# Seven block products for the last down projection of a float32 decoder trunk, its weight sums made by adding transfers

## The reference

```python
def swiglu_ffn(h, w_gu, w_down):
    g, u = jnp.split(h @ w_gu, 2, axis=-1)
    return (jax.nn.silu(g) * u) @ w_down
...
        x = x + 0.5 * swiglu_ffn(rmsnorm(x, n_ffn2[i]), ffn2_w_gu[i], ffn2_w_down[i])
    return rmsnorm(x, n_final)
```

## Time and profile before

| | us |
|---|---|
| median of 3 runs (1934.22 to 1935.02) | 1934.61 |
| the profiled execution | 1933.99 |
| its span, first to last instruction | 1932.2 |

### The profile page before, as it was taken

The page is one execution under the profiler, slowest core; times in us unless marked ns, Lnnn a source line. Parts: engine busy times, 40 slices in busy tenths (PEclk is TensorE's granted clock), DMA queues, the critical chain, the costliest instruction groups (busy, mean ns, idle before and its releaser), DMA issues.

```text
span 1932.2 us, 31908 instructions
## 1 busy us (share of the span) xinstructions
PE 1923.7 (100%) x12020; PEld 1740.5 (90%) x12020; DVE 1347.7 (70%) x2111; ACT 964.4 (50%) x1612; POOL 329.0 (17%) x331
## 2 busy tenths in 40 slices
PE   9999999999999999999999999999999999999998
PEld 7998998888898889989998998999898889989997
DVE  7865875687765658847866985687487569837854
ACT  7542554355554546524544653365356446524543
POOL 2200212100112121101201120121312123401200
PEclk9999999999999999999999999999999999999999
DMA  6734974323443627736943683695353427847932
GB/s 181 164 109 117 181 153 138 109 67 108 131 128 114 173 87 171 157 103 150 186 111 119 135 169 98 140 189 132 110 179 121 109 70 180 173 153 164 188 109 87
DMA packets 385097, 263.82 MB, mean 137 GB/s; under 512 B 19314, under 2 KB 367600, under 8 KB 384992
## 3 DMA queue, kind: packets, MB, share of 16 engines
q1 hardware_dynamic: 303840, 209.22, 36.4%
q0 software_dynamic: 72224, 51.19, 17.3%
q10 hardware_dynamic: 8928, 2.11, 0.5%
HBM read 251.99 MB, written 10.49 MB: 136 GB/s over the span
## 4 chain that ended last, share of the span: by engine, by line
PE 97%; DVE 1%; issue 1%; ACT 1%; DMA 0%; ACTq 0%
PE ps L434 19%; PE ps L435 18%; PE ps L436 18%; PE ps L1068 14%; PE ps L1067 14%; PE ps L1066 14%; DVE w_lo L2118 0%; ACT w_hi L1447 0%; PE ps L992 0%; PE ps L926 0%; DVE sums L2876 0%; DMA x_tok<-in_x 0%; DVE sums L2896 0%; DVE up L3065 0%; PE ps L1192 0%
## 5 line engine op out<-in xcount | busy, mean ns | idle before, releaser
L2118 DVE TENSOR_TENSOR w_lo<-raw,w_hi 128x512 fp32r<-128x512 f32 (+5 forms) x367 | 397.1, 1096 | 299.7 <-ACT w_hi L1447 299.3
L1447 ACT ACTIVATE w_hi<-raw 128x512 fp32r<-128x512 f32 (+5 forms) x367 | 342.6, 951 | 298.5 <-PE ps L436 255.1
L1067 PE MATMUL ps<-s_lo,w_hi 128*128 128x256 f32 x1248 | 353.2, 283 | 0.0
L1068 PE MATMUL ps<-s_hi,w_lo 128*128 128x256 f32 x1248 | 353.2, 283 | 0.0
L1066 PE MATMUL ps<-s_hi,w_hi 128*128 128x256 f32 x1248 | 353.2, 283 | 0.0
L1068 PE MATMUL ps<-h_hi,w_lo 128*128 128x256 f32 x936 | 264.9, 283 | 0.0
L1067 PE MATMUL ps<-h_lo,w_hi 128*128 128x256 f32 x936 | 264.9, 283 | 0.0
L1066 PE MATMUL ps<-h_hi,w_hi 128*128 128x256 f32 x936 | 264.8, 283 | 0.0
L1066 PEld LDWEIGHTS ps<-s_hi,w_hi 128*128 128x128 f32 x1248 | 239.6, 192 | 0.0
L1067 PEld LDWEIGHTS ps<-s_lo,w_hi 128*128 128x128 f32 x1248 | 239.6, 192 | 0.0
L1068 PEld LDWEIGHTS ps<-s_hi,w_lo 128*128 128x128 f32 x1248 | 239.6, 192 | 0.0
(11 more groups left out here) (406 smaller groups left out, 3789.8 us busy)
## 6 DMA issues: line engine op xcount, KB each, us to landing
raw<-in_ffn_w_gu SPq DMA_DIRECT2D x110, 512.0 KB, 5.0
raw<-in_ffn_w_down SPq DMA_DIRECT2D x36, 768.0 KB, 4.4
outer_even<-in_ffn_w_gu SPq DMA_DIRECT2D x70, 256.0 KB, 3.2
outer_even<-in_ffn_w_gu POOLq DMA_DIRECT2D x70, 256.0 KB, 5.4
raw<-in_ffn_w_gu SPq DMA_DIRECT2D x64, 256.0 KB, 6.1
raw<-in_x_w_kv SPq DMA_DIRECT2D x16, 1024.0 KB, 6.1
raw<-in_ffn_w_down SPq DMA_DIRECT2D x24, 640.0 KB, 4.2
outer_odd<-in_ffn_w_gu SPq DMA_DIRECT2D x54, 256.0 KB, 3.6
```

The source lines that it names most:

```text
L1067: nc.tensor.matmul(to, hi[:, kk, :], right_lo, start=False, stop=False, skip_group_check=True)
L1068: last = nc.tensor.matmul(to, lo[:, kk, :], right_hi, start=False, stop=kk == KH - 1, skip_group_check=True)
L1447: return nc.scalar.activation(out_ap, in_ap, ACT.Copy, **kw)
L2118: return nc.vector.tensor_tensor(out_ap, value, hi.bitcast(F32), ALU.subtract)
```

## The change

The last block's 20 mixed slots become one run, and its down projection comes once, behind them, as seven block products. The operands are split in two along tokens (256 and 256), rows (11 and 11) and columns (512 and 512); each product is 2 token tiles x 11 rows x 3 matmuls of 512 columns, cut in six tiles of two rows (the last of one). The gated values stay in float32 (mid); their forms are made as sums by VectorE and split tile by tile, four tiles ahead. The weight forms: P1, P2 and P3 are plain; P5, P6 and P4 take w_chain, to which POOL adds one block after the other by accumulating transfers of up to four rows; P7 takes P3's raw rows with one more addition. ScalarE copies P1's first eight rows into w_chain. Each product is taken into x by one to two scaled additions for each token tile (POSTS). The additions of POOL for slots l = 10 to 19 now follow the loads of x by token on its queue.

```diff
-    TOKEN_GROUPS = ((0, 3), (3, 3), (6, 3), (9, 2))
-    LAST_GROUP = len(TOKEN_GROUPS) - 1
+    RUNS = (2, 2, 2, 1)
...
+    DOWN_ORDER = (P1, P2, P5, P6, P3, P7, P4)
+    DOWN_GROUPS = ((0, 4), (4, 4), (8, 3))
+    DOWN_TILES = ((0, 2), (2, 2), (4, 2), (6, 2), (8, 2), (10, 1))
+    PER = len(DOWN_TILES)
+    LAST_TILE = PER * PRODUCTS
+    POSTS = {P1: ((0, 0, 1), (1, 0, 1)), P2: ((0, 0, -1), (1, 0, -1)), P5: ((2, 1, 1), (3, 1, 1)),
+             P6: ((0, 1, -1), (1, 1, -1)), P3: ((0, 1, 1), (1, 1, 1)),
+             P7: ((2, 1, -1), (3, 1, -1), (2, 0, 1), (3, 0, 1)), P4: ((2, 0, -1), (3, 0, -1))}
...
+    def run_slots(n, part):
+        return range(FC) if RUNS[n] == 1 else range(part * HALF, (part + 1) * HALF)
+
+    def first_mixed(n, part):
+        return max(run_slots(n, part)[0], PLAIN_FIRST[n])
+
...
+            w_chain = last_run.enter_context(nc.sbuf_tensor("w_chain", [P, HALF, SEQ], F32))
...
+        w_rest = region("w_rest", 32 * KB, [P, 3, SEQ])
+        final_gain = region("final_gain", 38 * KB, [P, D])
+        mid = region("mid", 44 * KB, [P, FC, SEQ])
+        first_hi_forms = region("first_hi_forms", 88 * KB, [P, 4, TH], F32R)
+        first_lo_forms = region("first_lo_forms", 92 * KB, [P, 4, TH], F32R)
...
+        DOWN_BANK = {P1: (4, 5), P6: (4, 5), P7: (4, 5), P2: (6, 7), P5: (0, 1), P3: (0, 1), P4: (2, 3)}
+        RAW_AT = {(P1, 0): 0, (P1, 1): 1, (P2, 0): 2, (P2, 1): 3, (P2, 2): 4, (P3, 0): 5, (P3, 1): 6}
...
+            def load_down_products():
                 down = io.ffn2_w_down[1].rearrange("(k p) n -> p k n", p=P)
-                for half in range(2):
-                    for g, (row, nrows) in enumerate(TOKEN_GROUPS):
-                        w = at["down", 3, part, half, g].slot
-                        first = part * HALF + row
-                        sp.wait_ge(sig.w_lo_ready, w - 1)
-                        sp.dma_start(wide(raw[:, w % 2])[:, 0:nrows, :],
-                                     down[:, first:first + nrows, half * SEQ:(half + 1) * SEQ])\
-                          .then_inc(raw_loaded[w % 2], 16)
+                def load_rows(i, g):
+                    k0, nrows = DOWN_GROUPS[g]
+                    first, half = k0 + (HALF if i in (P2, P3) else 0), int(i == P3)
+                    r = RAW_AT[i, g]
+                    sp.dma_start(rows_of(i, g), down[:, first:first + nrows, half * SEQ:(half + 1) * SEQ])\
+                      .then_inc(raw_loaded[raw_slot(r)], 16)
+                sp.wait_ge(sig.w_lo_ready, SLOTS - 1)
+                load_rows(P1, 0)
+                sp.wait_ge(sig.w_lo_ready, SLOTS)
+                load_rows(P1, 1)
+                sp.wait_ge(sig.product_done, PRODUCTS_DONE)
+                k0, nrows = DOWN_GROUPS[2]
+                sp.dma_start(w_chain[:, k0:k0 + nrows, :], down[:, k0:k0 + nrows, 0:SEQ]).then_inc(sig.t1_loaded, 16)
+                for g in range(2):
+                    sp.wait_ge(sig.w_lo_ready, SLOTS + tile(P1, 2 * g + 1) + 1)
+                    sp.wait_ge(sig.x_scaled_ready, CHAIN_COPIED + g + 1)
+                    load_rows(P2, g)
+                sp.wait_ge(sig.form_lo_ready, FORMS_DONE)
+                sp.wait_ge(sig.t1_loaded, REST_LOADED + 16)
+                sp.dma_start(w_rest[:], down[:, HALF + k0:HALF + k0 + nrows, SEQ:]).then_inc(sig.t1_loaded, 16)
+                for g, freed in enumerate((P2, P2, P2)):
+                    sp.wait_ge(sig.w_lo_ready, SLOTS + tile(freed, 2 * g + 1) + 1)
+                    if g == 0:
+                        load_rows(P2, 2)
+                    else:
+                        load_rows(P3, g - 1)
...
-                pool.dma_start(final_gain[:], io.n_final.unsqueeze(0).broadcast_to([P, D])).then_inc(sig.gain_loaded, 16)
...
+            def add_down_sums():
+                down = io.ffn2_w_down[1].rearrange("(k p) n -> p k n", p=P)
+                pool.wait_ge(sig.product_done, PRODUCTS_DONE)
+                pool.wait_ge(sig.form_lo_ready, FORMS_DONE)
+                pool.dma_start(final_gain[:], io.n_final.unsqueeze(0).broadcast_to([P, D])).then_inc(sig.gain_loaded, 16)
+                for g, (k0, nrows) in enumerate(DOWN_GROUPS):
+                    if g < 2:
+                        pool.wait_ge(sig.x_scaled_ready, CHAIN_COPIED + g + 1)
+                    else:
+                        pool.wait_ge(sig.w_lo_ready, SLOTS + tile(P1, 2 * g + 1) + 1)
+                    pool.dma_start(w_chain[:, k0:k0 + nrows, :], down[:, k0:k0 + nrows, SEQ:], accum_op=ALU.add)\
+                        .then_inc(CHAIN_ADDED[g][0], 16)
+                for g, (k0, nrows) in enumerate(DOWN_GROUPS):
+                    pool.wait_ge(sig.w_lo_ready, SLOTS + tile(P5, 2 * g + 1) + 1)
+                    pool.wait_ge(CHAIN_ADDED[g][0], CHAIN_ADDED[g][1] + 16)
+                    pool.dma_start(w_chain[:, k0:k0 + nrows, :], down[:, HALF + k0:HALF + k0 + nrows, SEQ:],
+                                   accum_op=ALU.add).then_inc(CHAIN_ADDED[g][0], 16)
+                for g, (k0, nrows) in enumerate(DOWN_GROUPS):
+                    pool.wait_ge(sig.w_lo_ready, SLOTS + tile(P6, 2 * g + 1) + 1)
+                    pool.wait_ge(CHAIN_ADDED[g][0], CHAIN_ADDED[g][1] + 32)
+                    pool.dma_start(w_chain[:, k0:k0 + nrows, :], down[:, HALF + k0:HALF + k0 + nrows, 0:SEQ],
+                                   accum_op=ALU.add).then_inc(CHAIN_ADDED[g][0], 16)
+                for g, (k0, nrows) in enumerate(DOWN_GROUPS):
+                    pool.wait_ge(sig.w_lo_ready, SLOTS + tile(P3, 2 * g + 1) + 1)
+                    pool.dma_start(rows_of(P3, g), down[:, k0:k0 + nrows, SEQ:], accum_op=ALU.add)\
+                        .then_inc(T3_ADDED[g][0], 16)
...
-            add_run(3, 1)
+            for l in range(C + 2, mixed_count(3, 0)):
+                add_outer(3, 0, l)
...
+            def down_products():
+                last_slot = len(mixed_slots) - 1
+                for k in range(LAST_TILE):
+                    i, q = DOWN_ORDER[k // PER], k % PER
+                    pe.wait_ge(sig.form_lo_ready, FORMS_DONE + k + 1)
+                    pe.wait_ge(sig.w_lo_ready, SLOTS + k + 1)
+                    if q == 0:
+                        if i == P2:
+                            pe.wait_ge(sig.mixed_dve_step, dve_step(last_slot, C11_TAKEN))
+                            pe.wait_ge(sig.mixed_act_step, act_step(last_slot, P5_TAKEN))
+                        if i in (P5, P4):
+                            pe.wait_ge(sig.mixed_dve_step, dve_step(last_slot, C21_TAKEN))
+                        if i in (P6, P3, P7):
+                            pe.wait_ge(sig.evacuated, evacuated_after({P6: P1, P3: P5, P7: P6}[i]))
+                    hi, lo = down_w(w_hi, k), down_w(w_lo, k)
+                    left_hi, left_lo = down_forms(first_hi_forms, s_hi, k), down_forms(first_lo_forms, s_lo, k)
+                    nrows = DOWN_TILES[q][1]
+                    for j in range(2):
+                        to, ts = ps[:, DOWN_BANK[i][j], :], slice(j * P, (j + 1) * P)
+                        for n in range(nrows):
+                            fresh = i in (P1, P2, P5, P4) and (q, n) == (0, 0)
+                            nc.tensor.matmul(to, left_hi[:, n, ts], hi[:, n, :], start=fresh, stop=False,
+                                             skip_group_check=True)
+                            nc.tensor.matmul(to, left_hi[:, n, ts], lo[:, n, :], start=False, stop=False,
+                                             skip_group_check=True)
+                            last = nc.tensor.matmul(to, left_lo[:, n, ts], hi[:, n, :], start=False,
+                                                    stop=(q, n) == (PER - 1, nrows - 1), skip_group_check=True)
                         last.then_inc(sig.part_done, 1)
...
+                        down_form_hi(0)
+                        down_hi(0)
...
+                    for k in (2, 3):
+                        down_form_hi(k)
+                    down_hi(2)
+                    high_silu(m, s)
+                    return
...
+            def down_products():
+                copied = {4: 0, 5: 1}
+                nc.scalar.activation(idle[:], eps[:], ACT.Sqrt)
+                down_hi(3)
+                for k in range(LAST_TILE):
+                    if k in copied:
+                        g = copied[k]
+                        k0, nrows = DOWN_GROUPS[g]
+                        act.wait_ge(sig.product_done, PRODUCTS_DONE)
+                        hi_part(w_chain[:, k0:k0 + nrows, :], rows_of(P1, g)).then_inc(sig.x_scaled_ready, 1)
+                    if k >= 4:
+                        down_hi(k)
+                    if k + 4 < LAST_TILE:
+                        down_form_hi(k + 4)
+                    if k == 18:
+                        for tt in (0, 1):
+                            token_squares(early(tt), tt, evacuated_after(P2) - 1 + tt)
+                    if k in (34, 35):
+                        tt = k - 34
```

(93 more changed lines are left out.)

330 lines of the change are left out of this document (201 added, 129 removed).

## The result

The changed kernel takes 1944.27 us (median of 5, 1942.74 to 1944.87) beside 1934.61 for the kernel before: 1.0048 times as long, 95% interval 1.0035 to 1.0062. It is **slower by 0.5%**, where 1929.1 was forecast, and the time lies 1.3 us above the range. The profiled execution has a span of 1942.6 us, 10.4 more than before.

The account below looks back on a forecast made before the run. It took TensorE, busy without a gap, as the bound: 66 fewer matmuls (-14.96) + 4.0 + 3.3 + 0 + 2.2 = -5.5 us, from a median of 1934.6 to 1929.1 us. Range 1923 to 1943.

Parts of the forecast that it names:

- Entering the down stage: Start of the down stage: PE stalls 1.3 at tile 4, 1.1 plus 0.9 at tile 6; 3.3 us, 1.5 to 6.
- Rival (2): As P2 begins: plain loads share engines packet by packet with additions, stalls 13.2 rather than 3.3 us; 1939; chance 0.11.
- Slot 9: Slot l = 9: additions for l = 10, behind x's loads, land at 1703.5 and stall PE 4.0 us, 1.5 to 6.
- Rival (4): Slot 9's pause: TensorE's clock falls, 3.5 us at 1.2 GHz costing about as much again; 1932.5; chance 0.10.
- Rival (3): Slot 9: the x loads do not hold the additions up, so the 4.0 us go; 1925.1; chance 0.15.
- The transfers' term: Additions from P5 on: 165 ns per 2 KB packet, hidden below 195, so 0 us; 16 us late at 256.
- Rival (1): Tiles 30 to 35: additions cost by byte, 256 ns a packet, and P7's chain falls behind; 1945; chance 0.17.
- VectorE: Down products: VectorE's work exceeds 14.96 by 1 to 3 us in P6 and P3, covered by four-tile lead; 0 us.
- The end: After PE's last matmul: tokens 2 and 3 end only 3 matmuls apart, token 3 taken later; +2.2 us, 1.5 to 3.

Follow-up runs that it names:

- no_first_sums: Changed kernel with P5's three first additions into w_chain cut to 16 columns of one row each (P5, P6, P4 multiply other weights): 1930.41 us.
- rest_late: Changed kernel with w_rest's 768 KB load issued behind P3's loads instead of between P2's second and third: 1937.86 us.
- x_late: Changed kernel with the additions for slot l = 10 issued ahead of the loads of x instead of behind them: 1937.91 us.
- no_later_sums: Changed kernel with the nine additions for P6, P4 and P7 cut to 16 columns of one row each (these multiply other weights): 1943.62 us.
- ahead_early_p3: Changed kernel with l = 10 additions ahead of x, w_chain loaded directly, P2's first and last rows loaded earlier, P4's last tiles by token: 1927.99 us.
- direct_rest: Changed kernel with w_rest's load behind P3's, w_chain filled by loads instead of ScalarE's copies, P2's first two loads earlier: 1935.75 us.
- two_queues: Changed kernel with half of each of P2's first two loads issued by ScalarE on its own queue: 1941.86 us.
- wait_x_rest_tail: Changed kernel with P5's additions held for P2's first two loads, l = 10 additions ahead of x, w_rest behind P3's loads, P4's last tiles by token: 1932.68 us.

## Why the prediction was wrong

**The failed step is "Entering the down stage"**: 3.3 us forecast, 15.6 measured (11.7 of waits, counted from start to start of the matmuls, 3.9 of lower clock and restart). Its two stalls were right: 1.3 and 2.0 at tiles 4 and 6, measured 1.1 and 1.8, and of the second the additions made 0.7, by no_first_sums, where 0.9 was put. What it lacked stands two and four tiles further on, 5.1 and 3.7 us at tiles 8 and 10. I stopped at these 0.9 us for "the first addition into w_chain beside it", where the step should have followed every load of SyncE's queue up to P2's third: 1 MB, w_rest's 768 KB, 768 KB, each packet behind one of an addition.

**Rival (2) is what happened**, by its mechanism. That its 13.2 us of stalls came near the 11.7 us is partly luck: it put 6.2, 2.8 and 2.9 us at tiles 6, 8 and 10, where 1.8, 5.1 and 3.7 came, and it had no w_rest ahead of the third load, without which tile 10 did not wait (rest_late). I gave it 0.11, and the evidence I held against it was misread: raw loads of 4.9 and 4.7 us with and without additions are medians over stretches; in the first the additions' queue held the engines 40% of the time, in pieces of 256 KB, so many of a load's packets may have met none (I did not count them). A median over a mixed stretch can't speak for a megabyte beside a megabyte. Its 1939 fell short of 1944.27 mostly by the clock: 1.5 us in slot 9 and 3.5 in the stage.

**Slot 9** was right in place and size: 4.0 forecast, 3.65 measured and, by x_late, due to x; VectorE took the addition up at 1704.96 in an execution whose slots start 1.57 us later, so at 1703.4 by the time axis of before, where 1703.5 was put. Rival (4) came true beside it rather than instead of it: the clock fell behind this pause, for the 3.5 us that it put (no row of before showed that length), and this cost 1.5 us. Its price of 3.5 was reckoned wrong: a stretch at half the clock loses half its length, not as much again. The prediction let rivals (2) and (4) exclude each other, but a rival that makes pauses can bring the clock with it. Rival (3) is refuted.

**The transfers' term**, 0, was right in this kernel: 183 ns (165 taken, 195 the point where it turns), no gap in P6 and P7, and no_later_sums the same as after. Rival (1) is refuted at this price. The Trainium skill (Collectives: The Full Stack, "The bandwidth ceiling: the fold count and why AG ≠ RS ≠ AR") has the reduction of a collective ring read two sources where a copy reads one, at half the rate. Carried over to these additions, as the prediction did, that is an estimate of 2 x 92.4 = 185 ns, and the trace's 183 agrees. But the term looked only at the chain from P5 on, and that it held owes something to luck: with most of P2's waits gone, P5 and P6 come some 15 us earlier and PE waits there as well (ahead_early_p3).

**VectorE**, 0, held: no wait of PE in the fifth stretch, with VectorE busy for 64.6 of 74.7 us. **The end**, 2.2, was 2.0. **Not in the sum** were 1.0 us ahead of P4 in the last slot, which every variant shows. In the kernel after VectorE works without a pause from 1808.52 until it has made what P4 waits for, and two of its operations there are new, the low part of a first form and a sum into mid, 1.0 us together; what happens without them was not tried.

## What to carry to other kernels

When transfers that add are moved beside loads that a tensor engine waits for, write down every load on every queue with its size and its due time, and let them share packet for packet: a cheap load then moves at the dear one's pace. Order each queue by due time, and look for transfers that stand ahead of an urgent one for no reason (x ahead of the additions: 5 us; w_rest ahead of P2: 4.6 us). A pause can have a lower clock behind it, and not every pause has, so compare pauses and clock apart; and saved work counts only as far as the transfers that pay for it fit.

## What the runs showed of the hardware

- Two queues that both have work move equal numbers of packets (652 to 652 in 10 us), three as well (95, 98, 96 in 2 us), though a packet of an addition took 172 ns there (70.0% x 10 us x 16 / 652) and a plain one 96. A load split over two queues got two packets of three.
- An added transfer of 2 KB packets took 183 ns a packet on each engine, alone and for 43 us on end; plain ones took 92. Plain ones beside additions: 39.1% x 10 us x 16 / 652 = 96 ns.
- In the kernel after TensorE ran at 0.50 to 0.52 of its clock for 3 to 4 us behind pauses of 3.65, 5.1 and 3.7 us, which cost 1.5 to 2.0 us each time. The pause's length alone did not decide it: behind 3.4 us in slot 9 of direct_rest and 2.9 us at tile 8 of two_queues the granted clock was 1.00, behind 2.5 and 2.0 us in wait_x_rest_tail it fell. What decides it stays open.
